# Two tiles projected together, the folds in another order, and an earlier norm in the opening of a decoder-layer kernel

## What is computed

```
q, k, v, u = split(rmsnorm(x) @ w_in)           # w_in: 1024 x 2048
attn  = softmax(q1 k1) v - lambda * softmax(q2 k2) v   # 4 heads, causal, bucketed bias
attn  = rmsnorm(attn, per head) * 0.8
pool  = (windowed means of u - u) @ pool_w       # windows 2, 4, 8, 16
x    += concat(attn, pool) @ w_out
xn    = rmsnorm(x)
s     = (xn @ peer_wq) . peer_keys               # 8 heads x 2 halves x 128 keys
idx   = top 16 of the pair sums of the two top-16 lists
x    += sum over heads, k of softmax(top)_k * gelu(xn . u_tab[idx_k]) * v_tab[idx_k]
x    += sigmoid(rmsnorm(x) @ w_gate) * (p @ w_ple);  y = rmsnorm(x)
lambda = exp(lq1 . lk1) - exp(lq2 . lk2) + 0.2
```

## Time and profile before

| | us |
|---|---|
| median of the timed runs | 3205.69 (3203.79 to 3205.81) |
| the profiled execution | 3209.12 |
| its span | 3207.1 |
| TensorE busy | 2387.9 (74%) |
| VectorE busy | 2238.4 (70%) |
| ScalarE busy | 951.4 (30%) |
| GpSimd busy | 1325.4 (41%) |
| indirect fetches, share of the 16 DMA engines' span | 86.1% |

### The profile page before, as it was taken

How to read it: one execution, slowest core, us unless ns; L and a number is a source line. 1 busy time by engine, 2 the same in 40 slices (tenths; PEclk the granted TensorE clock), 3 DMA queues, 4 the chain that set the end, 5 groups by cost and what they waited for, 6 DMA issues and landing times.

```text
span 3207.1 us, 53243 instructions
## 1 busy us (share of the span) xinstructions
PE 2387.9 (74%) x20836; PEld 951.4 (30%) x20836; DVE 2238.4 (70%) x5463; ACT 951.4 (30%) x2428; POOL 1325.4 (41%) x1143
## 2 busy tenths in 40 slices
PE   8879999567877778757876767576678676767666
PEld 3643333223333333213432222122222221212112
DVE  1366667768878788756667667587777777777764
ACT  2212232325335344212322222132323232232222
POOL 0024444324334344435565544344444444444441
PEclk9989999888888889867788878788888887888877
DMA  6579999999999999999999999999999999999994
GB/s 262 184 289 421 421 412 419 417 417 390 418 392 406 416 417 416 413 409 418 417 415 412 416 417 394 418 411 420 408 414 407 420 419 421 404 419 407 421 420 183
DMA packets 202995, 1266.96 MB, mean 395 GB/s; under 512 B 24144, under 2 KB 27496, under 8 KB 61040
## 3 DMA queue, kind: packets, MB, share of 16 engines
q0 software_dynamic: 159808, 1133.76, 86.1%
q1 hardware_dynamic: 41500, 129.51, 10.2%
q10 hardware_dynamic: 1436, 0.29, 0.0%
HBM read 1235.00 MB, written 28.65 MB: 394 GB/s over the span
## 4 chain that ended last, share of the span: by engine, by line
DMA 30%; PE 15%; DVE 6%; POOL 3%; issue 3%; ACT 2%; DVEq 2%; POOLq 0%; ACTq 0%
DMA ring<-in_uv,idx 30%; PE sc L964 7%; DVE ring L1793 3%; PE sc L997 3%; POOL ring L1975 3%; PE route L939 1%; DVEq L1803 1%; PE sc L966 1%; ACT diag L1334 1%; PE work L985 0%; POOL front L1991 0%; ACT hgelu L1329 0%; PE sc L863 0%; PE sc L661 0%; PE sc L957 0%
## 5 line engine op out<-in xcount | busy, mean ns | idle before, releaser
L1975 POOL DMA_INDIRECT ring<-in_uv,idx x1056 | 1246.9, 1181 | 1655.0 <-PE sc L966 1417.6
L1793 DVE CUSTOM_DVE_ANT_0 ring<-ring,xn_cur 128x1024 f32<-128x1024 f32 x1056 | 1280.6, 1222 | 651.0 <-DMA ring<-in_uv,idx 646.4
L964 PE MATMUL sc<-ring,diag 32*32 32x512 f32 x8192 | 1240.8, 725 | 656.2 <-ACT diag L1334 607.9
L966 PE MATMUL sc<-ring,diag 32*32 32x512 f32 x8192 | 1240.9, 725 | 0.0
L964 PEld LDWEIGHTS sc<-ring,diag 32*32 32x32 f32 x8192 | 271.3, 118 | 1437.9 <-ACT diag L1334 1037.1
L1329 ACT ACTIVATE hgelu<-hdot 128x2 f32<-128x2 f32 x528 | 107.5, 204 | 1821.5 <-DVE hdot L1793 1820.5
L1334 ACT ACTIVATE diag<-gate_d,hgelu 128x32 f32<-128x32 f32 x1056 | 281.8, 314 | 21.2
L966 PEld LDWEIGHTS sc<-ring,diag 32*32 32x32 f32 x8192 | 270.6, 118 | 2.3 <-issue 2.3
L521 PE MATMUL sc<-big,front 128*128 128x512 f32 x448 | 209.0, 611 | 4.6 <-DVE front L1439 4.6
L1329 ACT ACT_TABLE_LOAD x128 | 164.2, 1283 | 2.3
L939 PE MATMUL route<-big,xnT 128*128 128x256 f32 x560 | 138.8, 403 | 0.0
(11 more groups left out here) (271 smaller groups left out, 2340.8 us busy)
## 6 DMA issues: line engine op xcount, KB each, us to landing
front<-wqk_scratch SPq DMA_DIRECT2D x27, 1024.0 KB, 13.1
ring<-in_uv,idx POOLq DMA_INDIRECT x1056
big<-in_w_in SPq DMA_DIRECT2D x8, 1024.0 KB, 14.4
wqk_scratch<-front SPq DMA_DIRECT2D x8, 1024.0 KB, 6.6
big<-wqk_scratch SPq DMA_DIRECT2D x8, 1024.0 KB, 22.5
x<-x_scratch SPq DMA_DIRECT2D x13, 512.0 KB, 8.8
front<-in_x SPq DMA_DIRECT2D x8, 512.0 KB, 8.1
xnT<-in_wq_t POOLq DMA_DIRECT2D x8, 512.0 KB, 4.8
```

The lines of the kernel that those rows point to most:

```text
L964: pe.matmul(sc[own, 0, :], diag[own, r, :], uv_rows[own, r, D:D + W4], start=opens_sum, stop=closes).then_inc(row_added[r], 1)
L966: pe.matmul(sc[other, 1, :], diag[own, r, :], uv_rows[own, r, D + W4:2 * D], start=opens_sum, stop=closes).then_inc(row_added[r], 1)
L1793: dve.tensor_tensor_reduce(uv_rows[:, k % RING, 0:D], uv_rows[:, k % RING, 0:D], xn_cur[:, :], 1.0, 0.0, ALU.mult, ALU.add, hdot[:, n % 2, ...
L1975: pool.indirect_dma_start(uv_rows[:, k % RING, :], None, uv, bass.IndirectOffsetOnAxis(ap=idx[:, n % PH, j:j + 1], axis=0)).then_inc(row_i ...
```

## The change

- LEAD is 18 instead of 19, so the opening has one slot less.
- SyncE loads x of tile 1 ahead of w_in. Tile 1 is turned in slot 0, and project_early takes the place of project_first and of tile 1's four project calls: for each block k of w_in, four matmuls of tile 0 into A0, A1, S0, S1 and four of tile 1 into WK, RT, TA, TB. It waits for both tiles' turns first. Tile 1's projection banks are emptied by VectorE (keep_second), in slot 0.
- On VectorE constants() is called ahead of the loop over slots, and its end is cut off into lam_constant() in slot 0; ScalarE's exponential for lambda moves ahead of its loop as well. The lambda vectors are loaded into xn_next.
- Band and pool of tile 0 come one slot sooner (1 and 2), tile 1's turn, band and pool in slots 1, 2 and 3. The slots of scores, weights, values, norms and outputs, counted from slot 0, stay.
- The folds begin in slot 3, one a slot up to slot 9, two in slots 10, 12, 13 and 14, one in slot 11; the heads with keys in the second half go first. The even pieces from the ninth on are staged in xn_cur, which held those keys, so xnT is free; piece 8's load waits for piece 7 instead of 6.
- The norm of the new x of tile 0 stays in slot 13, its turn goes to slot 14, and routes 0, 1 and 2 to slots 15, 16 and 17. load_weights(2) is now in slot 15, tile 1's stores of x1 stay in 16.

```
-LEAD = 19
+LEAD = 18
 def turn_x_slot(t):
-    return 10 * (t - EARLY) if t >= EARLY else -LEAD + t
+    return 10 * (t - EARLY) if t >= EARLY else -LEAD
-FOLD_HEADS = (2, 3, 4, 5, 6, 7, 0, 1)
+FOLD_HEADS = (4, 5, 6, 7, 2, 3, 0, 1)
 def fold_slot(j):
-    return -LEAD + (5 + j // 2 if j < 12 else j - 1)
+    return -LEAD + (3, 4, 5, 6, 7, 8, 9, 10, 10, 11, 12, 12, 13, 13, 14, 14)[j]
 def attention_slots(t):
     if t < EARLY:
-        b = -LEAD + (1, 4)[t]
+        b = -LEAD + 1
...
-        return Attention(None, None, b, b + 1, b + 2, ...
+        return Attention(None, None, b, b + t, b + t + 1, ...
 # TensorE, slot 0
+            def project_early():
+                for t in range(EARLY):
+                    for c in (TA, TB):
+                        pe.wait_ge(free[c], emptied(c, ("x", t)))
+                    for o in range(4):
+                        b = project_bank(t, o)
+                        pe.wait_ge(free[b], opens(b, ("project", t, o)))
                 for k in range(KD):
                     pe.wait_ge(w_in_in[k], 16)
+                    for t in range(EARLY):
+                        for o in range(4):
+                            b, at = project_bank(t, o), COLUMNS[o] * W4
+                            mm = pe.matmul(bank[b], xTp[t][:, k, :], w_in_sb[:, k, at:at + W4],
+                                           start=(k == 0), stop=(k == KD - 1))
+                            if k == KD - 1:
+                                mm.then_inc(ready[b], 1)
 # VectorE
+            def keep_second(o):
+                b = project_bank(1, o)
+                dve.wait_ge(ready[b], filled(b, ("project", 1, o)))
+                dve.tensor_scalar((B[1].q, B[1].k, B[1].u, B[1].v[1])[o], bank[b], st[:, XR + 1:XR + 2], None, ALU.mult
+                                  ).then_inc(free[b], 1)
+            constants()
             for s in range(-LEAD, 0):
                 front_step(s)        # in slot 0 it ends with lam_constant() and four keep_second(o)
-                if s == -LEAD:
-                    constants()
...
-                if s == ROUTE_0 - 3:
+                if s == ROUTE_0 - 2:
                     dve.wait_ge(late_in, 16 * 3)
                     norm_sum(0)
 # ScalarE
+            act.wait_ge(lam_sum, 2)
+            act.activation(st[:, LAME:LAME + 2], st[:, LAMS:LAMS + 2], ACT.Exp).then_inc(lam_exp, 1)
             for s in range(-LEAD, 0):
 # GpSimd
-                    pool.wait_ge(ready[A1], filled(A1, ("fold", j - 2)))
+                    pool.wait_ge(ready[A1], filled(A1, ("fold", j - 1 if j == PH else j - 2)))
-                pool.dma_start(wq_st[j % 2], wq_t[hp * T:(hp + 1) * T, :]).then_inc(wq_in[j % 2], 16)
+                pool.dma_start(wq_st(j), wq_t[hp * T:(hp + 1) * T, :]).then_inc(wq_in[j % 2], 16)
 # SyncE
             load_x(0)
+            load_x(1)
             for k in range(KD):
                 load_w_in(k)
-            load_x(1)
```

More of the change, by code:

```diff
@@ L61, in turn_x_slot @@
 def turn_x_slot(t):
-    return 10 * (t - EARLY) if t >= EARLY else -LEAD + t
+    return 10 * (t - EARLY) if t >= EARLY else -LEAD
 def project_slot(t, o, half):
-    return 10 * (t - EARLY) + 2 + 2 * o + half if t >= EARLY else -LEAD + t * (1 + o)
+    return 10 * (t - EARLY) + 2 + 2 * o + half if t >= EARLY else -LEAD
 def kept_slot(t, o):
@@ L99, in attention_slots @@
         end = values[-1]
-        return Attention(None, None, b, b + 1, b + 2, [(0, (t + 1) * T)], scores, weights, weights, values,
+        return Attention(None, None, b, b + t, b + t + 1, [(0, (t + 1) * T)], scores, weights, weights, values,
                          (end + 1, end + 1), end + 2, (end + 3, end + 4))
@@ L235, in front_and_experts, with wq_st @@
                    xn_cur[:, :].rearrange("p (a b) -> p a b", b=NK)]
-        wq_st = [xnT[:, :, :].rearrange("p a b -> p (a b)"), cut(ring_a, 14848, D)]
+        def wq_st(j):
+            if j % 2:
+                return cut(ring_a, 14848, D)
+            return xnT[:, :, :].rearrange("p a b -> p (a b)") if j < PH else xn_cur[:, :]
         stage = [cut(fr, i * 2048, KD, 256) for i in range(2)]
@@ L248, in front_and_experts @@
         junk_x = cut(fr, 10240, W4).bitcast(bf16)
-        lam_in = cut(fr, 7680, 4, QK)
+        lam_in = xn_next[:, 0:4 * QK].rearrange("p (a b) -> p a b", b=QK)
         strip_sbuf = [cut(fr, 8192 + i * W4, W4) for i in range(H)]
@@ L367, in project_bank @@
         def project_bank(t, o):
-            return (A0, A1, S0, S1)[o] if t == 0 else ((A0, A1) if t < EARLY else (S0, S1))[o % 2]
+            if t < EARLY:
+                return ((A0, A1, S0, S1), (WK, RT, TA, TB))[t][o]
+            return (S0, S1)[o % 2]
         def band_bank(t):
@@ L686, in front_step @@
                 if s == -LEAD:
-                    project_first()
-                for t in range(NT):
-                    if t and s == turn_x_slot(t):
+                    pe.wait_ge(x_in[1], 16)
+                    turn_x(1, xt[1])
+                    project_early()
+                for t in range(EARLY, NT):
+                    if s == turn_x_slot(t):
                         pe.wait_ge(x_in[t % 2], 16 * (t // 2 + 1))
                         turn_x(t, xt[t % 2])
-                    for o in range(4 if t else 0):
+                    for o in range(4):
                         for part in range(2):
@@ L1026, in fold_keys @@
                         mm = pe.matmul(bank[b][:, k * NK:(k + 1) * NK],
-                                       wq_st[j % 2][:, (4 * c + k) * T:(4 * c + k + 1) * T],
+                                       wq_st(j)[:, (4 * c + k) * T:(4 * c + k + 1) * T],
                                        keys_sb[hp // PH][:, hp % PH, :], start=True, stop=True)
@@ L1109, in keep @@
                 act.wait_ge(ready[b], filled(b, ("project", t, o)))
-                to = (B[t].q, B[t].k, B[t].u, B[t].v[t])[o] if t < EARLY else kept[o]
+                to = (B[0].q, B[0].k, B[0].u, B[0].v[0])[o] if t == 0 else kept[o]
                 act.activation(to, bank[b], ACT.Copy, scale=st[:, XR + t % 2:XR + t % 2 + 1]).then_inc(free[b], 1)
@@ L1214, in front_step @@
                     for o in range(4):
-                        if s == kept_slot(t, o):
+                        if t != 1 and s == kept_slot(t, o):
                             keep(t, o)
@@ L1405, in constants, with lam_constant @@
                 dve.tensor_scalar(pidx[:, :], pagef, float(PAGE), row, ALU.mult, ALU.add).then_inc(page_idx, 1)
+            def lam_constant():
                 dve.wait_ge(lam_exp, 1)
@@ L1409, in constants @@
                 dve.tensor_scalar(st[:, NLAM:NLAM + 1], st[:, SNM:SNM + 1], LAM_INIT, None, ALU.subtract)
+                dve.drain()
             def keep_fold(j):
@@ L1586, in front_step @@
                         x_factor(t)
+                if s == -LEAD:
+                    lam_constant()
+                    for o in range(4):
+                        keep_second(o)
                 if s == SAMPLE_NORM:
```

3 lines of the change are left out of this document (removed).

## The result

The changed kernel took 3220.88 us (median of 5, 3220.22 to 3225.3) against 3205.81 for the kernel before in the same session: ratio 1.0045, 95% interval 1.0034 to 1.0056, so 15.1 us slower. A second session with the unaltered kernel gave 1.0051 (1.0037 to 1.0065), 3223.78 against 3207.81. Forecast were +12.0 and a range of 3204 to 3226. The profiled execution took 3225.3, its span is 3223.3. Ratios and intervals are of the undisturbed executions: one of the nine of experiment 3 took 4365 us (the others 3210 to 3219), for which nothing here gives a reason, and is left out of its ratio.

The account below looks back on a forecast made before the run. An opening up to the first fetch, then a stretch bound by DMA bytes: first fetch +14.5, less 2.5 for 1 MB moved ahead of it, +12.0 us, 3217.7 by the timed runs' measure; range 3204 to 3226.

Parts of the forecast that it names:

- The border at the first fetch: First expert-row fetch, at 190.98 us before: a microsecond on it is one on the total; bytes bound all behind.
- Part 1: Start of the opening: VectorE waits for the constants first, so projection starts at 35.3 us, 14.6 later.
- first come, first served: DMA order that would let x of tile 1 delay the constants by 1.2 us; going round the queues gives 0.
- Part 2: Early projection: eight banks save nothing, passes stay 0.43 us apart; both tiles take 57.2 us.
- Part 3: Slots from projection's end to first fetch: 113 us, putting the fetch at 205.5, +14.5.
- E: Instant the early projection of both tiles ends, forecast at 92.5 us.
- The sooner route wins nothing: End of the opening: route 0 ahead of tile 1's output gains nothing, as the fetch waits for that output.
- Part 4: load_weights(2) moves ahead of the first fetch: 1 MB out of the full stretch, 2.5 us back.
- A: Rival, chance 0.13: the start isn't late, constants land early or their wait hides; -1.3, 3204.4 us.
- B: Rival, chance 0.07: folds' stretch shrinks, no wq load stalls, clock stays up, slots 4 to 9 close up; -8.5, 3197.
- C: Rival, chance 0.08: nothing comes back from load_weights(2), output halves run slow, constants slip 1.2; +20, 3225 us.
- D: Rival, chance 0.04: slots 4 to 9 are bound elsewhere and stay at 5.5 us; +9 more, 3227 us.

Follow-up runs that it names:

- experiment 3: Changed kernel with fold piece 8 in slot 11 instead of 10, behind half an output projection; ratio 1.0020 to the kernel before.
- experiments 1: Changed kernel with constants() and ScalarE's exponential of lambda put back behind the two x evacuations of slot 0; 3210.73 us, ratio 1.0012.
- experiment 2: Kernel before with only constants() and ScalarE's exponential moved ahead of the slots; 3212.66 us, ratio 1.0022.
- experiment 8: Changed kernel with the same eight banks, but all of tile 0's projection matmuls ahead of tile 1's; ratio 1.0044.
- experiment 9: Changed kernel with LEAD at 19 again, so norm, turn of xn and routes move one slot back; 3224.41 us, ratio 1.0045.
- experiment 4: Changed kernel with load_weights(2) one slot later on SyncE, behind the store of x1 of tile 1; 3226.17 us, ratio 1.0062.
- experiment 6: Changed kernel with fold piece 8 in slot 11 and four places for peer_wq blocks from piece 8 on; 3208.76 us, ratio 1.0004.

## Why the prediction was right, step by step

**The border at the first fetch.** Held. Over thirteen profiles of eleven programs first fetches lie from 180 to 213 us, and the stretch behind stays within 3004 to 3016.

**Part 1, the constants: +14.6 at the start.** Measured 14.97 (20.66 to 35.63). That it was the wait's place in VectorE's list, and not w_in, the turn or the landing, is shown by experiments 1 and 2 from both sides. On first come, first served against round the queues: VectorE goes on behind the last constant at 28.64 to 29.06, mean 28.9, in the ten profiles with x of tile 1 ahead of w_in, and at 28.42 to 28.61, mean 28.5, in the three without. So x ahead of w_in cost it 0.4, nearer to the 0 that followed from the Trainium skill (DMA: Bandwidth & Descriptors, Queues, rings and completion order) than to 1.2.

**Part 2, eight banks save nothing.** The block took 57.8 us (forecast 57.2), and experiment 8 shows nothing won by the order by block. No run changes the number of banks alone; for it speaks that the passes start 0.43 us apart with eight banks as they did with four. By that spacing the Trainium skill's line on eight banks (Perfetto Trace Analysis, Matmul Optimizations) had nothing to win here: the stream was dense with four.

**Part 3, E to the first fetch: 113.** Measured 119.9 and 117.0 from the block's end at 93.5 and 93.7 in the two profiles. Slots 1 to 9 were right within half a microsecond (10.5 forecast to the end of fold 0, 10.5 measured; 35.6 forecast to the end of fold 6, 35.3 measured), and so was the wait for piece 8 (5.0, measured 5.18 and 5.34). Over the four profiles with this opening, slots 10 to 12 took 40.3 to 40.9 us instead of 39.0, slots 13 and 14 up to route 0 took 18.9 to 21.9, mean 19.9, instead of 17.2, and route 0 to the fetch 21.8 instead of 21.1.

The term that was too small above all is the loads of slots 13 and 14: forecast were waits of 3.0 ahead of piece 12 and 2.5 ahead of 14, 5.5 together, and 13 and 15 on time. Measured were 2.07, 3.70 and 3.08 ahead of 12, 13 and 15, 8.9 together (7.3 in the second profile), none ahead of 14. Two things went into it. I had used the median landing of 4.7 for every piece, but the load of 13, issued 2 us behind that of 12 and 0.5 ahead of SyncE's store of a folded head (170.51), lands 7.5 us after its issue (6.8 in the second profile, 6.4 in experiment 3); whether the store, the load before it or both slowed it no run shows. And the load of 15 waits for fold 13, one fold earlier: it was issued at 181.51, right behind that fold's end, and landed 5.0 later, with only a turn and fold 14 to cover it. The forecast had counted this for pieces 12 and 14 and left it out for 15.

The slow passes behind the waits came to about their sum, but elsewhere: fold 12, taken at 3.4, took 2.05, and fold 13, taken at 2.0, took 3.68 (3.21 in the second profile). Fold 7 (3.62), fold 8 (3.78 where 3.4 was taken) and the output behind it (7.64 to 8.21 where 7.4 was taken) are the excess of slots 10 to 12. Of the last 0.7, the fetch was issued 0.9 us behind the end of the output, which the sum had at nothing.

The first fetch was therefore 22.4 us later in the first profiles and 18.6 in the second ones, against 14.5 forecast; the means are 210.6 (four) and 191.5 (two), 19.1 apart.

**The sooner route wins nothing.** Borne out by the traces of experiment 9, and by its time within 4 us. The fetch is released by the output, as forecast, and the indices are ready at 205.1, 8 us ahead.

**Part 4, 2.5 us back.** The mean stretch of the eight profiles with load_weights(2) ahead of the fetch is 3009.2 (3003.9 to 3011.8), of the five with it behind 3012.2 (3009.3 to 3016.1): 3.0 back, though single profiles in a group differ by 7 to 8 us. Closer to the border the scatter is smaller: the 33rd fetch comes 88.7 to 89.4 us after the first in the eight and 91.1 to 93.1 in the five, means 89.0 and 91.7. So 2.7 us were back within the first 92, where 2.5 were forecast. That it is the megabyte's transfer and not TensorE's wait for it is argued from the size alone; a wait that starved the ring from its first refill would have moved the ninth fetch, and it doesn't in experiment 4.

**The sum.** With means of the profiles that share an opening, 210.6 (four) less 191.5 (two) is 19.1, less 3.0 is +16; the times say 15.1 and 16.0. The forecast of +12 was some 4 us short: 0.8 in start and block, 1.6 in slots 10 to 12, 2.7 in slots 13 and 14 and 0.7 ahead of the fetch, less 0.3 in slots 1 to 9, 0.5 by which the mean first fetch of before lies above 190.98, and 0.5 more that came back. The two mechanisms, the late start and the megabyte back, came near their sizes. Inside slots 13 and 14 there was some luck: a wait of 2.5 ahead of piece 14 that never came made up for most of one of 3.1 ahead of piece 15 that was not forecast.

**The rivals.** A fell with the start at 35.63. B named the right lever for a gain: with the loads' waits gone the kernel is 13 to 15 us faster than the changed one (experiment 6). That is less than B's price of 20.5, since slots 4 to 9 didn't close up and the banks' emptying took the place of part of the waits. It didn't happen because the change itself puts fold 8 in the slot of fold 7. C and D were in their direction half right: the stretch was dearer, in slots 10 to 14 and not in 4 to 9. (D's +9 doesn't follow from its own numbers: six slots of 5.5 are 33.0, 7.9 more than the 25.1 counted.)

## What to carry to other kernels

Before moving a wait to the head of an engine's list, read what stood in front of it: a wait that was free behind an evacuation delayed TensorE by 12.0 us ahead of it in experiment 2, of which 9.1 reached the first fetch, and in the changed kernel one call's place was 10.6 of 15 us. When work is packed closer, compute again which buffer each load waits for: one piece a slot gave what it promised until two pieces stood in a slot, and a load was issued only a fold or less before it was needed. And in a kernel with a full stretch behind an opening, the instant of the first big transfer is the number to predict, but take it from more than one profile when 5 us matter.

## What the runs showed that I had not expected

- One profile's first fetch scatters by 4.5 us for one and the same opening (208.85, 209.61, 210.64, 213.37 us), through landing times and the clock behind waits: the half output behind fold 8 took 8.21, 8.05, 7.64 and 7.69 us.
- A fetch released by a matmul was issued 0.8 us after VectorE had already begun on the same bank (213.37 and 212.59); one released by the indices 0.3 us after them (190.98 and 190.71). What the difference is, the profile doesn't say.
- In experiment 2 the delay shrank by itself, from 12.0 us at the first projection to 7.9 at the first band: a late start also took away the waits and the slow start that stood behind the old one.
